# Routed experts: low part of the down weights in two halves, on GpSimd and on VectorE

## The reference

```python
def swiglu(x, w_gate, w_up, w_down):
    return (jax.nn.silu(x @ w_gate) * (x @ w_up)) @ w_down
...
    def block_fn(args):
        tok, w, e = args
        return swiglu(x_pad[tok], we_gate[e], we_up[e], we_down[e]) * w[:, None]
```

## Time and profile before

| | us |
|---|---|
| median of 3 runs | 2818.81 (2818.26 to 2821.91) |
| the profiled execution, its own time | 2823.84 |
| its span | 2822.1 |
| TensorE busy | 2591.8 (92%) |
| VectorE busy | 1587.0 (56%) |
| GpSimd busy | 1471.3 (52%) |
| ScalarE busy | 1145.8 (41%) |

### The profile page before, as it was taken

How to read it: one execution, slowest core, us unless ns; L and a number is a source line. 1 busy time by engine, 2 the same in 40 slices (tenths; PEclk the granted TensorE clock), 3 DMA queues, 4 the chain that set the end, 5 groups by cost and what they waited for, 6 DMA issues and landing times.

```text
span 2822.1 us, 49123 instructions
## 1 busy us (share of the span) xinstructions
PE 2591.8 (92%) x11208; PEld 1859.5 (66%) x11209; DVE 1587.0 (56%) x2591; ACT 1145.8 (41%) x1534; POOL 1471.3 (52%) x1756
## 2 busy tenths in 40 slices
PE   6999997996899998899999999999999999999980
PEld 2754663522456666688777788888777877777760
DVE  6379977994577667334333343445445554454425
ACT  4232312223323332344444444455555555555532
POOL 2002205225466665354555555566777677766756
PEclk8999999997999999999999999999999999999995
DMA  8152604373323321867777777788888998889877
GB/s 273 64 97 90 212 5 64 134 244 135 128 90 105 111 84 61 288 160 184 198 198 200 210 196 222 207 238 266 256 259 263 278 280 259 258 251 279 254 205 271
DMA packets 304951, 534.60 MB, mean 189 GB/s; under 512 B 38597, under 2 KB 204485, under 8 KB 304120
## 3 DMA queue, kind: packets, MB, share of 16 engines
q1 hardware_dynamic: 250248, 352.77, 38.0%
q0 software_dynamic: 51472, 173.70, 25.8%
q10 hardware_dynamic: 3168, 7.34, 0.7%
HBM read 395.75 MB, written 138.00 MB: 189 GB/s over the span
## 4 chain that ended last, share of the span: by engine, by line
PE 26%; issue 20%; POOL 12%; POOLq 9%; DVE 2%; DMA 1%; ACT 0%; SPq 0%; ACTq 0%; DVEq 0%
PE psm L1090 19%; PE psm L1036 4%; POOL arena L2180 3%; POOL arena L2177 3%; POOL st L2170 2%; POOLq L2176 2%; POOLq L2198 2%; PE psm L1083 2%; POOLq L2197 1%; POOLq L2189 1%; POOL arena L2190 1%; POOL st L2054 1%; POOL acc_d L2194 1%; POOL st L2202 1%; POOL st L2053 1%
## 5 line engine op out<-in xcount | busy, mean ns | idle before, releaser
L1090 PE MATMUL psm<-whi,xhi 128*128 (+1 forms) x1424 | 575.6, 404 | 29.0 <-issue 17.6
L1090 PE MATMUL psm<-whi,xlo 128*128 (+1 forms) x1424 | 558.6, 392 | 0.0
L1090 PE MATMUL psm<-wlo,xhi 128*128 (+1 forms) x1424 | 557.3, 391 | 0.0
L1929 DVE TENSOR_TENSOR arena<-psm,arena 128x256 f32<-128x256 f32 x178 | 75.5, 424 | 599.7 <-ACT arena L1457 593.8
L1764 DVE SCALAR_TENSOR_TENSOR arena<-arena,cw 128x1024 f32<-128x1024 f32 x240 | 335.8, 1399 | 8.6
L2185 POOL TENSOR_TENSOR wlo<-raw,whi (+1 forms) x64 | 330.6, 5166 | 19.1 <-ACT whi L1489 19.1
L1090 PEld LDWEIGHTS psm<-whi,xhi 128*128 128x128 f32 x1424 | 268.6, 189 | 100.8 <-issue 49.7
L1090 PE MATMUL psm<-whi,hhi 128*128 (+1 forms) x712 | 295.6, 415 | 19.5 <-POOL wlo L2185 13.4
L2194 POOL DMA_INDIRECT acc_d<-arena x162 | 278.7, 1720 | 58.4 <-issue 54.0
L1090 PEld LDWEIGHTS psm<-whi,xlo 128*128 128x128 f32 x1424 | 268.7, 189 | 59.0
L1090 PEld LDWEIGHTS psm<-wlo,xhi 128*128 128x128 f32 x1424 | 269.2, 189 | 51.3
(11 more groups left out here) (359 smaller groups left out, 3951.2 us busy)
## 6 DMA issues: line engine op xcount, KB each, us to landing
raw<-in_we_gate_dram SPq DMA_DIRECT2D x64, 1024.0 KB
raw<-in_we_up_dram SPq DMA_DIRECT2D x64, 1024.0 KB
raw<-in_we_down_dram SPq DMA_DIRECT2D x64, 1024.0 KB, 5.2
arena<-in_w_ada_dram SPq DMA_DIRECT2D x12, 2048.0 KB
arena<-in_x_dram SPq DMA_DIRECT2D x32, 512.0 KB, 5.5
h_d<-arena SPq DMA_DIRECT2D x17, 512.0 KB, 9.0
arena<-in_w_in_dram SPq DMA_DIRECT2D x16, 512.0 KB, 6.6
mix_d<-bo SPq DMA_DIRECT2D x32, 256.0 KB, 2.3
```

The lines of the kernel that those rows point to most:

```text
L1090: m = TE.matmul(o, a, w, start=(n == 0), stop=(n == len(todo) - 1))
```

## The change

Half of the low down weights (the second 1024 columns of the 2048) goes from GpSimd to VectorE. VectorE has a function of its own for it, `split_low_down`, which waits for the same cast and raises a new semaphore, `s_wlod_ready`. It is called at the end of VectorE's step, behind `h_low`, under the flag that GpSimd has used so far; for this VectorE reads the flag and the expert's ordinal of its own block, two more value_loads in every step. Ahead of the loop it is called for the first two experts. TensorE waits for both semaphores before `down`, and the SP queue before it loads the next down weights.

```diff
--- before.py
+++ after.py
@@ -248,6 +248,7 @@
         s_wgate_in = sem("wgate_in")
         s_wup_in = sem("wup_in")
         s_wlow_ready = sem("wlow_ready")
+        s_wlod_ready = sem("wlod_ready")
         s_wdown_in = sem("wdown_in")
         s_ob_full = sem("ob_full")
         s_sqm_ready = sem("sqm_ready")
@@ -711,6 +712,7 @@
                 SY.dma_start(gu[:, :, 1, :], up.rearrange("(k p) f -> p k f", p=P)).then_inc(s_wup_in, 16)
                 if split is not None:
                     sp.wait_ge(s_wlow_ready, split)
+                    sp.wait_ge(s_wlod_ready, split)
                 if number is not None:
                     sp.wait_ge(s_wdown_in, number)
                 SY.dma_start(raw[:, bass.ds(base + WG, FE * D)].rearrange("p (k f) -> p k f", k=FE),
@@ -798,6 +800,7 @@
                 if i == 0:
                     sp.wait_ge(s_wlo_ready, nexp)
                     sp.wait_ge(s_wlow_ready, nexp)
+                    sp.wait_ge(s_wlod_ready, nexp)
                 SY.dma_start(xps[i], x1_d[i * P:(i + 1) * P, :]).then_inc(s_xp_in, 16)
 
             nb = sp.value_load(nbi[0:1, 0:1], min_val=TOPK, max_val=NB)
@@ -1199,6 +1202,7 @@
                 gate_up(b, ((o + 1) & 1) * WSLOT)
                 turn_rows(b + 1, 1 - w)
                 pe.wait_ge(s_wlow_ready, q)
+                pe.wait_ge(s_wlod_ready, q)
                 down(b - 1, ((q + 1) & 1) * WSLOT)
                 turn_h(b)
 
@@ -1946,7 +1951,15 @@
                            whi[:, bass.ds(slot + c * GC, GC)], ALU.subtract)
                 m.then_inc(s_wlo_ready, 1)
 
+            def split_low_down(slot, number):
+                dve.wait_ge(s_whid_ready, number)
+                half = slot + WG + FE * D // 2
+                tt(wlo[:, bass.ds(half, FE * D // 2)], raw[:, bass.ds(half, FE * D // 2)],
+                   whi[:, bass.ds(half, FE * D // 2)], ALU.subtract).then_inc(s_wlod_ready, 1)
+
             def routed_step(b):
+                f = dve.value_load(splits[0:1, bass.ds(b - NT, 1)], min_val=0, max_val=1)
+                o = dve.value_load(ordi[0:1, bass.ds(b - NT, 1)], min_val=1, max_val=E)
                 fn = dve.value_load(splits[0:1, bass.ds(b - (NT - 1), 1)], min_val=0, max_val=1)
                 on = dve.value_load(ordi[0:1, bass.ds(b - (NT - 1), 1)], min_val=1, max_val=E)
                 c = dve.value_load(berow[0:1, bass.ds(b + (3 * P - NT), 1)], min_val=0, max_val=NCOL - 2)
@@ -1955,6 +1968,8 @@
                 with dve.If(fn > 0):
                     split_low((on & 1) * WSLOT, on * NGC)
                 h_low(b)
+                with dve.If(f > 0):
+                    split_low_down((o & 1) * WSLOT, o + 1)
 
             squares_joined(0)
             ssn(0)
@@ -2013,7 +2028,9 @@
             hidden(NT, tabl[:, bass.ds(c, 1), 1])
             rows_low(NT + 1)
             h_low(NT)
+            split_low_down(0, 1)
             split_low(WSLOT, NGC)
+            split_low_down(WSLOT, 2)
             dve.wait_ge(s_br_ready, 1)
             fn = dve.value_load(splits[0:1, 1:2], min_val=0, max_val=1)
             with dve.If(fn > 0):
@@ -2182,8 +2199,8 @@
             def split_low(slot, number):
 
                 pool.wait_ge(s_whid_ready, number)
-                PO.tensor_tensor(wlo[:, bass.ds(slot + WG, FE * D)], raw[:, bass.ds(slot + WG, FE * D)],
-                                 whi[:, bass.ds(slot + WG, FE * D)], ALU.subtract).then_inc(s_wlow_ready, 1)
+                PO.tensor_tensor(wlo[:, bass.ds(slot + WG, FE * D // 2)], raw[:, bass.ds(slot + WG, FE * D // 2)],
+                                 whi[:, bass.ds(slot + WG, FE * D // 2)], ALU.subtract).then_inc(s_wlow_ready, 1)
 
             def add_block(b, w):
                 c = pool.value_load(berow[0:1, bass.ds(b + (3 * P - NT), 1)], min_val=0, max_val=NCOL - 2)
```

## The result

The changed kernel takes 2933.35 us (median of 4 runs, 2925.64 to 2933.67) against 2818.53 for the kernel before on the same chip: ratio 1.0381, 95% interval 1.0345 to 1.0417. It is slower by 110 us in the two profiled spans (2931.9 less 2822.1), not by the 62 forecast. The direction was right, the size was not.

What follows compares the result with a forecast made beforehand. TensorE was taken to bound the routed stage; terms 20 + 46 + 3 + 10 - 15 - 3 + 1 = +62 us on the profiled 2823.84 gave 2885.8, or 2881 against the median; range 2850 to 2925.

Steps and rivals of the forecast that it cites:

- the slack that the prediction gives to an odd step: In steps with the loop's turn, 0.3 us was taken as free between L1925's end and the next gate_up.
- Steps that split nothing, 0: In steps without weight splits, VectorE's two added loads and branch end before hidden starts, so they cost 0.
- Steps with a gate/up split alone, +20: In 36 such steps VectorE's added loads delay hidden and the next gate_up, 0.57 us in 27, 0.2 in 9: 20 us.
- Steps with both splits, 26 x 1.75 = 46: In 26 steps VectorE waits for the down cast with five loads behind it, delaying gate_up: 46 us, bounds 15 and 75.
- Down split alone, +3: In 36 such steps the cast ends early and VectorE's loads end hardly later than today: 3 us, bounds 0 and 20.
- the -15 of GpSimd's waits: Halving GpSimd's subtraction removes TensorE's 14 waits, 13.4 us, and 1.6 more by overlap with the transposes: -15 us.
- Slow loads, +10: Some VectorE register loads last far longer and fall into the steps with splits: 10 us, between 0 and 50.
- Rival (b): Slow loads meet the critical place as a rule, 0.8 us in all 62 steps that split: +102 us; chance 0.17.
- That the wait holds the queue behind it: VectorE's semaphore wait for the down cast holds the next step's value_loads; first load 0.42 us after release.
- Rival (c): VectorE's wait for the cast holds nothing behind it: 31 us less than forecast, +31 us; chance 0.09.
- VectorE's half "runs beside the loads, so it adds nothing": VectorE's down half, 128 x 1024, lasts 1.22 us beside its register loads and adds nothing to the sum.
- TensorE's second wait and the SP queue at 0: TensorE's extra wait before down is covered by queued matmuls; the down load starts 2 us earlier, nothing waits: 0 each.

Runs made afterwards that it cites:

- e6: The kernel before with one more unused register load of TensorE at each turn of its loop (80 turns): 2915.73 us, ratio 1.0307.
- e2: The kernel before with the two new value_loads added to VectorE's step, their registers unused, and nothing else: 2897.21 us, ratio 1.0251.
- e8: The kernel before with TensorE's second register load moved behind gate_up and turn_rows: 2822.31 us, ratio 0.9974.
- e18: The changed kernel with TensorE's second register load moved behind turn_rows, nothing else: 2875.32 us, ratio 1.0187 against the kernel before.
- e1: The kernel before, but in the loop GpSimd subtracts only half of the low down columns and nobody the rest: 2853.87 us, ratio 1.0108.
- e4: The changed kernel with VectorE's down half one step later, so it waits for no cast; five loads stay ahead of hidden: 2872.88 us, ratio 1.0166 against before.
- e15: e1 plus a GpSimd padding operation behind the half; only the load of the next down weights waits for the padding's end: 2833.07 us, ratio 1.0017.
- e14: e1 plus a GpSimd padding operation behind the half; only TensorE's down waits for the padding's end: 2863.34 us, ratio 1.0126.
- e19: The changed kernel with GpSimd's scatter index copied ahead of the landing wait, nothing else: 2904.41 us, ratio 1.0288 against the kernel before.
- e3: The changed kernel with VectorE's two new loads behind rows_low; half and wait stay at the step's end: 2863.63 us, ratio 1.0155 against the kernel before.
- e5: The changed kernel with VectorE's two new loads behind rows_low and its down half one step later, ahead of h_low: 2875.49 us, ratio 1.0175 against before.
- e10: The kernel before with GpSimd's scatter index copied ahead of the landing wait, alone: 2844.67 us, ratio 1.0063.
- e12: The kernel before with GpSimd's scatter index copied ahead of the landing wait and TensorE's second load behind turn_rows: 2783.72 us, ratio 0.9835.

## Why the prediction missed

The step that failed is the slack that the prediction gives to an odd step: "in the step before, L1925 ends at 1390.38, and gate_up could have begun at 1390.79 instead of 1391.13", and hidden 0.43 ahead of L1925 besides. Two chains end at gate_up. The one that the prediction follows goes over L1925. The second goes from hidden's end over turn_h's wait to the loop's turn and two register loads of TensorE: in the odd step at 1381.46 hidden ends at 1388.72 and gate_up starts 2.41 later. This chain has no slack for hidden in an odd step. e6, e2 and the odd steps of e8 show it, and e18 gives the price of one of its two loads in the changed kernel: 1.9% of the 3.8%, two thirds of it in the odd steps. In an even step the chain is about 1.87 long (from the step at 1405.81, with both loads at 0.31), and becomes the longer one as soon as hidden is late.

By the terms of the sum, with the classes of the table:
- Steps that split nothing, 0: measured +18. In the even ones 21 of TensorE's loads are slow (one before). In the odd ones hidden ends 7.74 behind gate_up's start instead of 7.26: 31 of VectorE's loads there are slow (5 before), so they were not hidden. No run isolates either.
- Steps with a gate/up split alone, +20: measured +27, but for another reason: in the odd ones hidden ends 0.76 later and the step is 0.83 longer, so all of the delay arrives. Slow loads have hardly a part in it (three in the 31 steps).
- Steps with both splits, 26 x 1.75 = 46: measured +64. VectorE's part was rather too large (in the step worked out L1930 ends 9.96 behind gate_up's start, not 10.64, since the cast ends 3.47 behind it, not 4.21; in the 21 even steps 9.88 to 11.05, mean 10.26). TensorE's part was missing: in these 21 hidden ends 1.67 later than before and gate_up follows it another 0.75 later, and in each of the 21 one of TensorE's loads is slow. Taking one load out (e18) shortens them by 0.2 only.
- Down split alone, +3, with the -15 of GpSimd's waits: measured +9 instead of -12. The waits went; most of the 15 stretches at half clock follow a step with both splits and lie here (the step behind 1343.3 is 12.15 long).
- GpSimd's half was taken at 2.6 us and lasts 2.97, without effect. That it would only help was wrong by itself (e1), not in the changed kernel, where ScalarE's wait for it fell from 37.0 to 18.1, probably because longer steps leave the scatter time.
- Slow loads, +10, taken as chance: they are bound to a place (below). Rival (b), +102, was the nearest of the cases in size by luck: it put them on VectorE in the steps with splits, where 3 of VectorE's 52 lie, while 30 of TensorE's 53 do.
- That the wait holds the queue behind it is confirmed: the first load begins at 1410.0, 0.4 behind the start of the half, and without the wait the kernel is 2.1% faster (e4). Rival (c), and with it the rule of the Trainium skill's page "Perfetto Trace Analysis" (the section on the instruction's life cycle), by which the sequencer goes on to the next instruction while one waits, does not hold for VectorE here: register loads do not run ahead of a waiting subtraction. The cleaner case for the rule is h_low, whose own instruction waits: in all 96 waits ahead of it in the kernel before, the sequencer's next record begins 13 to 15 ns behind its start. The wait for the cast stands on a register operation ahead of the half (L1957, at 1409.32), so that the sequencer itself waits there.
- VectorE's half "runs beside the loads, so it adds nothing": nothing was said of what GpSimd does to it. Collisions are a term that the prediction did not have. They cost the changed kernel little (5 us), and its single parts more.
- TensorE's second wait and the SP queue at 0: nothing speaks against the first; the second was wrong in kind. An earlier down load costs 26 us between e1 and e15, and 30 between e14 and e15. In the changed kernel its share stays open: e19 takes 26 us off, by ScalarE's 18 us of waits and by fewer slow loads of TensorE (30 instead of 53), and no run parts the two.

The range ended at 2925, 8 below the median, because only one slow thing at a time was allowed for. Three were missed that meet in the same steps: TensorE's loads, the clock behind a gap, and the place of the slow loads.

## What to carry to other kernels

Before adding to a queue that "has slack", follow every chain that ends at the bounding engine's next instruction, its own sequencer's register loads behind its last wait included; the chain with the shorter visible tail may be the one without slack. Put register loads that nothing needs yet behind the work that the others wait for, on TensorE too. See whether two engines' operations that never met before will now run at the same time, and read the maximum of their durations, not the median. And when an edit frees a buffer earlier, look at which transfer that lets start and what has to land beside it.

## What the runs showed of the hardware

- A register load (TENSOR_LOAD) takes 0.30 us, or 0.5 to 1.7. In the traces of five of the kernels (before, after, e1, e2, e3), of those on VectorE, ScalarE and TensorE that had no gather issued within 4.5 us ahead, 508 of 1208 were over 0.5 us if they started 2 to 5 us behind the issue of GpSimd's accumulating scatter, and 2 of 2765 at any other time. Of 4298 that started over 5 us behind a scatter, at whatever time behind a gather, 2 were. So whether a load can be slow is a question of the scatter's place in the step; even in that place more than half are not. This and the collisions are probably why single edits gave -4 and +15 and both together -46; no run parts the two.
- VectorE's subtraction of two SBUF tiles did not run beside GpSimd's. In the traces of the changed kernel, e2, e4, e5, e6, e8, e10 and e12, 103 of VectorE's `wlo` subtractions lasted 1.6 to 7.0 us instead of 1.22, all while a split of GpSimd ran, and each ended 1.08 to 1.10 us behind it. VectorE's operations that read PSUM kept their durations beside it (hidden 0.42, `xlo` 1.22).
- Behind a stretch of 12.7 us in which TensorE idled for 3, its granted clock was 0.51 over the next 6.1 us (1.2 of 2.4 GHz); in the 1560 us of the stage before it never left 1.00.
- GpSimd's subtraction takes 2.97 us for 128x1024 and 5.19 for 128x2048: half the columns are 57% of the time.
- An accumulating scatter of 128 rows of 4 KB lands in about 6 us alone and mostly in 9.1 to 10.9 beside about 2 MB of weight loads.
